# Feeding the first layer of a two-block transformer with x by columns and its first weights in pieces

## What is computed

```python
h = rmsnorm(x, norm_g[l])        # x / rms(x) * g, per token
proj = h @ w_in[l]               # 256 x 1024 by 1024 x 4096
q_a = proj[..., 0:A]; k_a = proj[..., A:2 * A]; v_a = ...; g_a = ...
q_b = proj[..., o_b:o_b + Bw]; ...
```

## Time and profile before

| | us |
|---|---|
| median of 3 runs (lowest, highest) | 1177.98 (1177.89, 1178.29) |
| the profiled execution's own time | 1177.49 |
| its span in the profile | 1175.7 |
| TensorE busy in the span | 1155.3 |
| VectorE busy | 835.9 |
| ScalarE busy | 583.2 |
| GpSimd busy | 562.9 |

### The profile page before, as it was taken

One profiled execution on the slowest core, in us unless ns is written; L12 is line 12 of the kernel. 1 busy time (PEld: TensorE's weight loads), 2 busy tenths in 40 slices (PEclk: granted clock), 3 DMA queues, 4 the chain that ended last, 5 costly groups with the idle time before them and its releaser, 6 DMA issues.

```text
span 1175.7 us, 15187 instructions
## 1 busy us (share of the span) xinstructions
PE 1155.3 (98%) x5640; PEld 945.4 (80%) x5640; DVE 835.9 (71%) x1179; ACT 583.2 (50%) x764; POOL 562.9 (48%) x417
## 2 busy tenths in 40 slices
PE   9999999999999999899999999999999999999998
PEld 6787787877788888888887888888888887888887
DVE  7897578966897797678779667797793666654423
ACT  5557564676543442644343277443442756443440
POOL 1366324584364452734535228665351553545360
PEclk9999999999999999999999999999999999999999
DMA  9976479846799997569898568798874534876550
GB/s 353 354 274 225 135 252 332 277 161 223 238 368 319 342 347 273 187 216 343 276 338 319 218 234 283 245 346 300 321 277 142 197 115 161 268 245 193 207 197 36
DMA packets 183832, 297.91 MB, mean 253 GB/s; under 512 B 8464, under 2 KB 102352, under 8 KB 183760
## 3 DMA queue, kind: packets, MB, share of 16 engines
q1 hardware_dynamic: 177696, 284.82, 70.2%
q10 hardware_dynamic: 6064, 12.14, 3.1%
HBM read 294.79 MB, written 2.13 MB: 253 GB/s over the span
## 4 chain that ended last, share of the span: by engine, by line
PE 83%; DVE 8%; ACT 4%; issue 2%; SPq 1%; DMA 1%; POOL 1%; ACTq 0%; DVEq 0%
PE ps L1903 25%; PE ps L1916 25%; PE ps L1908 25%; PE ps L2196 2%; PE ps L1996 2%; DVE w_lo L1232 1%; ACT w_hi L665 1%; DVE ps L1216 1%; DMA raw<-w_in 1%; PE ps L2053 1%; POOL stat L525 1%; SPq L492 1%; PE ps L2042 1%; DVE ps L1328 1%; DVE x L1329 1%
## 5 line engine op out<-in xcount | busy, mean ns | idle before, releaser
L534 POOL TENSOR_TENSOR w_lo<-raw,w_hi 128x512 fp32r<-128x512 f32 x348 | 485.0, 1426 | 419.0 <-ACT w_hi L665 419.0
L665 ACT ACTIVATE w_hi<-raw 128x2048 fp32r<-128x2048 f32 x188 | 354.5, 1910 | 100.1 <-PE ps L1916 65.3
L1903 PE MATMUL ps<-w_hi,h_hi 128*128 128x512 f32 x1120 | 312.1, 400 | 1.1 <-issue 0.8
L1916 PE MATMUL ps<-w_lo,h_hi 128*128 128x512 f32 x1120 | 301.6, 391 | 1.6 <-DVE w_lo L1232 1.0
L1908 PE MATMUL ps<-w_hi,h_lo 128*128 128x512 f32 x1120 | 300.3, 390 | 0.0
L1232 DVE TENSOR_TENSOR w_lo<-raw,w_hi 128x2048 fp32r<-128x2048 f32 x96 | 224.7, 2346 | 100.5 <-ACT w_hi L665 98.4
L1916 PEld LDWEIGHTS ps<-w_lo,h_hi 128*128 128x128 f32 x1120 | 209.1, 188 | 50.0 <-DVE w_lo L1232 3.3
L1908 PEld LDWEIGHTS ps<-w_hi,h_lo 128*128 128x128 f32 x1120 | 210.2, 188 | 45.7 <-DVE h_lo L1292 0.2
L1903 PEld LDWEIGHTS ps<-w_hi,h_hi 128*128 128x128 f32 x1120 | 201.8, 188 | 43.5 <-issue 5.5
L1216 DVE SCALAR_TENSOR_TENSOR ps<-ada_raw,ccol,ps 128x512 f32<-128x512 f32 x240 | 181.1, 754 | 7.9 <-DMA ada_raw<-ada_w 1.1
L956 ACT ACTIVATE a_hi<-ps 128x512 fp32r<-128x512 f32 x44 | 26.4, 599 | 153.8 <-PE ps L2196 153.8
(11 more groups left out here) (208 smaller groups left out, 963.6 us busy)
## 6 DMA issues: line engine op xcount, KB each, us to landing
raw<-ffn_in SPq DMA_DIRECT2D x176, 512.0 KB, 5.9
ada_raw<-ada_w SPq DMA_DIRECT2D x144, 512.0 KB, 7.1
raw<-ffn_out SPq DMA_DIRECT2D x44, 1024.0 KB, 6.0
raw<-w_in SPq DMA_DIRECT2D x31, 1024.0 KB, 7.9
raw<-w_out SPq DMA_DIRECT2D x8, 1024.0 KB, 5.1
ada_raw<-kv_ada_w SPq DMA_DIRECT2D x16, 512.0 KB, 8.0
raw<-w_kv SPq DMA_DIRECT2D x8, 1024.0 KB, 5.8
raw<-w_q SPq DMA_DIRECT2D x4, 1024.0 KB, 5.1
```

The costliest lines, as they stand in the source:

```text
L534: ins = pool.tensor_tensor(w_lo[:, u % RAW, piece], raw[:, u % RAW, piece], w_hi[:, u % RING, piece].bitcast(F32), ALU.subtract)
L665: act.activation(w_hi[:, u % RING, :], raw[:, u % RAW, :], ACT.Copy).then_inc(*S.inc("w_hi_ready", u))
L1903: pe.matmul(bank(b), hi[:, k_in_lhs + k, tok], wh[:, k, c * 512:(c + 1) * 512], start=start and k == 0, stop=False)
L1916: ins = pe.matmul(bank(b), hi[:, k_in_lhs + k, tok], wl[:, k, c * 512:(c + 1) * 512], start=False, stop=stop and k == nk - 1)
```

## The change

x comes a second time from the host, transposed (`x_cols`, 1024 x 256), and is loaded straight as rows of the product: `x_T`, eight blocks of 128 x 256, lies in the buffer of `hn`. The transposes of x, their PSUM traffic and the warm-up between them go; there are four warm-up products in a row. Unit 0 is loaded in four pieces of 128 weight rows, each from the second on followed by its x columns; the first x columns are issued on ScalarE's queue between the norm's columns and the identity, which has a semaphore of its own. The columns of blocks 4 to 7 follow in one load, then unit 1 in two pieces. High and low parts are made by pieces. TensorE multiplies by pieces too, each for both tiles (`opening_unit`). x by rows, now needed for the squares and the residual only, is loaded behind unit 3. VectorE makes all of unit 0's low part. ScalarE makes the squares behind units 2 and 3 and writes them to another buffer. The half-root is computed ahead of the low part of unit 4.

The core of the diff:

```diff
-WARM_UP = (3, 1)
+WARM_UP = 4
+FIRST_PIECES = ([(k, k + 1) for k in range(4)], [(0, 2), (2, 4)])
...
+        x_T = hn.rearrange("p t d -> p (t d)").rearrange("p (k c) -> p k c", k=KC)
...
-        first_consts = [(ident[:], identity), (gcols[:], norm_cols)]
+        first_consts = [(gcols[:], norm_cols)]
...
-            sp.dma_start(x[:, 0, :], x_in[0:P, :]).then_inc(x_in_sem[0], 16)
+            def x_columns(i, a, z):
+                rows = x_cols[a * P:z * P, :].rearrange("(k p) n -> p k n", p=P)
+                sp.dma_start(x_T[:, a:z, :], rows).then_inc(x_cols_in[i], 16)
...
-                if u == 0:
-                    for k in range(0, 4, 2):
-                        sp.dma_start(into[:, k:k + 2, :], parts[0][:, k:k + 2, :]).then_inc(
-                            raw_in[0] if k else half_in, 16)
+                if u < 2:
+                    for i, (a, z) in enumerate(FIRST_PIECES[u]):
+                        landed = piece_in[u][i] if i < len(FIRST_PIECES[u]) - 1 else raw_in[u]
+                        sp.dma_start(into[:, a:z, :], parts[0][:, a:z, :]).then_inc(landed, 16)
+                        if u == 0 and i:
+                            x_columns(i, i, i + 1)
...
                 if u == 0:
-                    sp.dma_start(x[:, 1, :], x_in[P:2 * P, :]).then_inc(x_in_sem[1], 16)
+                    x_columns(4, 4, KC)
+                if u == 3:
+                    for t in range(NT):
+                        sp.dma_start(x[:, t, :], x_in[t * P:(t + 1) * P, :]).then_inc(x_in_sem[t], 16)
...
-                    low_first(0)
...
+            act.dma_start(x_T[:, 0, :], x_cols[0:P, :]).then_inc(x_cols_in[0], 16)
+            act.dma_start(ident[:], identity).then_inc(ident_in, 16)
...
+                for i in range(4):
+                    high_piece(0, i)
                 act.wait_ge(first_in, N_FIRST)
...
+                act.wait_ge(x_cols_in[4], 16)
+                for i in range(2):
+                    for k in (4 + 2 * i, 5 + 2 * i):
+                        act.activation(h_hi[:, k, :], x_T[:, k, :], ACT.Copy, scale=scale[:, k:k + 1]).then_inc(
+                            *S.inc("h_hi_cols", k))
+                    high_piece(1, i)
+                done[0] = 2
+                fill(3)
...
+                for k in range(4):
+                    dve.wait_ge(x_cols_in[k], 16)
+                    dve.tensor_scalar(h_hi[:, k, :], x_T[:, k, :], scale[:, k:k + 1], None, ALU.mult).then_inc(
+                        *S.inc("h_hi_cols", k))
+                    low_cols(k)
+                    low_piece(0, k)
+                for i in range(2):
+                    low_cols(4 + 2 * i)
+                    low_cols(5 + 2 * i)
+                    low_piece(1, i)
+                low_done[0] = 2
+                lows(3)
...
+            def opening_unit(u, b):
...
+                for i, (a, z) in enumerate(FIRST_PIECES[u]):
+                    pe.wait_ge(*S.at("w_hi_piece", u, i))
+                    for k in range(a, z):
+                        pe.wait_ge(*S.at("h_hi_cols", 4 * u + k))
+                        for t in range(NT):
+                            pe.matmul(bank(b + t), h_hi[:, 4 * u + k, t * P:(t + 1) * P], wh[:, k, :],
+                                      start=u == 0 and k == 0, stop=False)
...
+                else:
+                    ins.then_inc(*S.inc("unit_used", u))
+                    pe.wait_ge(ident_in, 16)
...
-                if layer == 0:
-                    norm_T(name, 0)
-                    warm_up(WARM_UP[1])
```

## The result

The changed kernel's median is 1182.36 us (1182.12 to 1182.78) against 1177.98 before: a ratio of 1.0037, with a 95% interval of 1.0026 to 1.0049. That is slower by 4.4 us where 4.5 were forecast. The number is right, and its account is not: in the changed kernel the steps that the prediction added up are hidden behind another one.

The account below looks back on a forecast made before the run. The prediction took TensorE as the bound, with unit 4's landing setting q's transposes early on. It summed 1177.49 + 2.9 - 0.1 + 0 + 1.7 = 1182.0, plus 0.5 to the median: 1182.5 us, range 1179.6 to 1184.6.

Parts of the forecast that it names:

- Term 1: Loads ahead of unit 4: x by columns adds 1.05 MB, so unit 4 lands 2.9 us later, at about 24.4.
- Term 2: From unit 4's landing to q's transposes: same path, half-root moved ahead saves 0.1 us; transposes start at 31.9.
- Term 3: Opening, costed at nothing: products from 6.5 to 6.8, unit 1 done at 17.8, later 5.9 us idle before q's transposes.
- Term 4: After the idle stretch before q's transposes: TensorE's clock falls to half, costing 1.7 us (bounds 0 and 2.2).
- The rigid shift after 32 us: After q's transposes all engines stand as before, only later; both traces run at a constant distance of 4.5 us.
- a sign that the prediction had named for being wrong: Behind 60 us: the prediction is wrong if the distance between the two traces shrinks there.
- the clock that holds: Rival: the clock stays at full speed through the gap before q's transposes, giving 1180.8 us; chance 0.09.
- rival (c): TensorE's 2.9 us gain up to unit 1's end is kept, with q's transposes ready at 26.0: 1175.1 us; chance 0.04.

Follow-up runs that it names:

- split one: Changed kernel with VectorE counting its four h_hi blocks on a semaphore of its own, apart from ScalarE's; 1183.55 us, ratio 1.0047.
- stretch filled: The split one with six products of zeros in TensorE's wait before the first transposes of q; 1180.93 us, ratio 1.0029.
- added bytes: Kernel before, with one more 1.05 MB load ahead of unit 4 into a free buffer, its data unused; 1180.08 us, ratio 1.0023.
- both edits: Changed kernel with VectorE's own semaphore count and q's evacuation put ahead of unit 4's high part on ScalarE; 1179.9 us, ratio 1.0022.
- lambda work moved: Kernel with both edits, plus lambda work and unit 4's low part put behind k's evacuation and q's copy, modulation work later; 1185.85 us, ratio 1.0069.

## Why the prediction came out as it did

**Term 1, the bytes (+2.9), right in kind, undersized, and hidden.** Unit 4 landed at 25.13 in the changed kernel, 25.26 in the split one, 24.77 with the stretch filled and 24.70 with the added bytes, that is 3.2 to 3.8 us later, against 2.9 forecast and an upper bound of 3.2. The term priced the new rows at 366 GB/s and left all others at 384; the whole stretch moved at 372 to 378. The added megabyte alone moved the transposes by 3.23 us and the medians by 2.3. In the changed kernel itself TensorE arrived after this path, so it didn't set the time; with the clock held it did again, 0.5 us behind TensorE.

**Term 2, the path behind it (-0.1), right.** High part, low part, lambda, evacuation, transposes: 25.26 to 32.84 in the split kernel is 7.58 us, against 7.67 before.

**Term 3, the opening costed at nothing, is the step that failed.** It had products from 6.5 to 6.8, unit 1 done at 17.8 and an idle stretch of 5.9 us ahead of the transposes. The changed kernel had products from 13.16, unit 1 done at 26.9 and no idle stretch there at all. The step costed each block's operations (0.35, 0.48 and 0.69 us in the trace, against 0.3, 0.5 and 0.6) and when each load lands. It didn't ask what a wait for `h_hi_cols` counts. Both increments of that name, by ScalarE and by VectorE, stand in the diff that the prediction quotes, and a waiter on one semaphore that two engines count on sees only their sum, so the order in which the counts were given out decides whom it waits for. Without the shared count the step holds: products from 6.56 (with the evacuation moved) or 7.66, unit 1 done at 17.9 or 19.0, and a wait of 5.56 us before the transposes.

**Term 4, the clock (+1.7), right in kind, undersized.** It fell in an idle stretch of 6.1 us instead of 5.9, at 12.2 us instead of 32, and stood at 0.50 for 6.8 us where 3.4 were taken from the earlier trace rows. It took 2.5 us of TensorE's time in the changed kernel, of which 2.1 reached the transposes (0.6 to 1.0 in the medians), and 2.6 in the split kernel, above the bound of 2.2. The lower level lasted longer than in the row it was sized by.

**The rest.** The rigid shift after 32 us held: 5.8 us at 65 and 5.9 at 489. The distance itself was 5.9 us instead of the constant 4.5 that was forecast, and it shrank to 5.3 behind 490 us, a sign that the prediction had named for being wrong; this was the low clock, which came in one profiled execution and not in the other. The medians differ by 4.4, since the profiled run of before lay 0.5 us below its median and that of the changed kernel (1182.78) 0.4 above. Of the rivals, the clock that holds (1180.8) is near what the filled stretch gave, 1180.93, with a larger delay of unit 4 than it assumed. The gain of 2.9 us (1175.1) failed for the reason given against it, and for one more that wasn't seen: even with the evacuation off the path, as rival (c) asked, VectorE's path to the first row maxima still hangs on unit 4 and brings attention's output 3.2 us late (1179.9).

So the sum was right because the late start and the forecast wait are substitutes. TensorE loses some 6 us of idle time and a slow clock either ahead of its first product or ahead of the transposes; the split kernel and the changed one differ by 1.2 us only, and by a time that the prediction had no reason to call. That 4.4 met 4.5 so closely is luck: where the forecast mechanism ran undisturbed, in the split kernel, its terms came to 3.7 and 2.6 us at the transposes, 6.3 in the spans and 5.8 in the medians. This is a right number by a partly wrong account. What is left open: the shared count seems to make the kernel 1.2 us faster than the split one (intervals of the ratios 1.0026 to 1.0049 and 1.0034 to 1.0061 overlap). The two traces are 0.5 us apart at attention's output and 1.0 in the spans, since behind 490 us the clock fell in that of the split kernel only; no run separated the rest. Not tried was a version with less VectorE work ahead of the first row maxima, or one that makes the squares from x by columns and so drops the second load of x.

## What to carry to other kernels

Before a product is costed as "ready when its block is ready", look at which engines count on the semaphore it waits for and in which order the counts were given out; two engines on one count make the first block wait for the other engine's last. A lead is worth only what the next meeting point of the engines lets through. If the engine with the lead already waits there in the trace of before (0.7 us at 59.41 here), follow the other engines' path to that point first, ahead of any sum about the opening: here it was VectorE's, and it hung on the same late load. And when an idle stretch can't be closed, products of zeros in it may be worth more than the edit (2.6 us here).

## What the runs showed of the hardware

- The same wait of 2.27 us was followed by a granted clock of 0.50 for 3.4 us in the trace of before and by 1.00 in that of the changed kernel (six of the eleven traces fell, five held), so a wait of that length is not a safe sign either way. In the idle stretches of 5.56 us (split kernel) and 6.1 us (changed kernel) the clock fell before TensorE took up work again, and it was low for 6.8 us in each.
- The four warm-up products at the start took 5.67 us in one trace (both edits) and 6.78 in another of the same opening (split kernel), with the column at 1.00 in both, and the first product came 1.1 us later for it (6.56 and 7.66).
- A VectorE operation on a single column (line 1423 in the kernel with the lambda work moved, rows above) took 1.21 us at 34.60 and 0.16 at 36.45. GpSimd's timeline of that kernel holds one piece of work in this stretch, the low part of a unit, which ends in between, at 35.80. The whole chain of such operations took 6.67 us there against 3.05 in the kernel before, where GpSimd had no work in it. What of GpSimd's work slows it was not tested.

```profile
30.69 5.11 POOL L548 TENSOR_TENSOR w_lo<-raw,w_hi 128x512 fp32r<-128x512 f32 x4 [8.03 <-ACT w_hi L678]
```
